# One tuned kernel for two transformer layers: convolution taps spread over three stages, the first merge chunk in the attention's drain, squares rounded on ScalarE

## What is computed

```python
def first_block(x, ...):
    h = rmsnorm(x, norm1_g)
    u, v_a, q, k, v_b = split(h @ w_in)
    y_a = chunked_spatial_gating(u, v_a, ...)
    o = diff_attention(q, k, v_b, lam, slopes)          # 8 heads, two maps each
    y_b = rmsnorm(o, sub_norm_g) * (1.0 - lam_init)     # over 128 elements of a head
    g_a, g_b = split(sigmoid(h @ w_gate + b_gate))
    x = x + (g_a * (y_a @ w_up_a) + g_b * (y_b @ w_up_b)) @ w_out
    return x + hierarchical_moe(rmsnorm(x, norm2_g), ...)   # 32 experts, 2 of them a token

def hybrid_layer(x, mem, ...):
    q_nsa, kv_nsa, g_nsa, conv_in, q_mem, g_merge = split(rms_norm(x, norm_mix) @ w_in)
    # NSA: compressed blocks (kc, vc), selected blocks, window; q_nsa normalised by head
    kc = rms_norm(compress_blocks(k_c, ...), nsa_qk_norm[1])
    o_nsa = nsa_attention(q, kc, vc, ks, vs, kw, vw, sigmoid(g_nsa))
    # convolution over time, 31 taps, each channel by itself
    u = a * sigmoid(ag)
    u = depthwise_conv(u, conv_w, 31 taps) + conv_b
    br_conv = silu(layer_norm(u, ...)) @ w_conv_out
    # attention to 256 memory rows, 4 heads of 128
    br_mem = softmax(qm @ km.T * 128 ** -0.5) @ vm @ w_mem_out
    gm = sigmoid(g_merge)                               # three gates of width 1024
    h = x + (gm[0] * br_nsa + gm[1] * br_conv + gm[2] * br_mem) @ w_out
    hn = rms_norm(h, norm_ffn)
    return h + (silu(hn @ w_gate) * (hn @ w_up)) @ w_down
```

## Time and profile before

| what | us |
|---|---|
| median of three executions (lowest, highest) | 1798.85 (1795.72, 1800.32) |
| the execution that was profiled, its own time | 1797.08 |
| span of that profile, first to last instruction | 1795.5 |
| TensorE busy in it | 1752.4 |
| VectorE, GpSimd, ScalarE busy | 877.8, 752.6, 579.6 |
| mean granted clock of TensorE, as a share of full speed | 0.991 |

### The profile page before, as it was taken

One profiled execution on the slowest core, in us unless ns is written; L12 is line 12 of the kernel. 1 busy time (PEld: TensorE's weight loads), 2 busy tenths in 40 slices (PEclk: granted clock), 3 DMA queues, 4 the chain that ended last, 5 costly groups with the idle time before them and its releaser, 6 DMA issues.

```text
span 1795.5 us, 22939 instructions
## 1 busy us (share of the span) xinstructions
PE 1752.4 (98%) x8545; PEld 1308.2 (73%) x8545; DVE 877.8 (49%) x1322; ACT 579.6 (32%) x1084; POOL 752.6 (42%) x623
## 2 busy tenths in 40 slices
PE   9999999998999999999999899999999999999999
PEld 6888877776887444443688677777788788888887
DVE  4221886667663244332552679997467442112211
ACT  2323445544233111111241345555462222212220
POOL 4444434334450000000341468887635545544442
PEclk9999999999999999999999999999999999999999
DMA  6322232224343899999722422221354223222221
GB/s 230 101 83 94 83 100 71 89 89 147 103 144 130 282 403 369 389 401 383 285 87 64 148 82 81 73 71 53 106 199 148 94 85 103 94 94 94 97 91 47
DMA packets 82935, 264.25 MB, mean 147 GB/s; under 512 B 9360, under 2 KB 10384, under 8 KB 82832
## 3 DMA queue, kind: packets, MB, share of 16 engines
q1 hardware_dynamic: 64608, 230.31, 36.5%
q10 hardware_dynamic: 15920, 28.32, 4.5%
q0 software_dynamic: 2304, 4.20, 0.7%
HBM read 249.16 MB, written 17.83 MB: 149 GB/s over the span
## 4 chain that ended last, share of the span: by engine, by line
PE 87%; DVE 9%; DMA 2%; ACT 1%; issue 1%; POOL 1%; SPq 0%; ACTq 0%; POOLq 0%; DVEq 0%
PE psum L620 84%; DVE area L2131 2%; DMA more<-stream 1%; DVE area L2190 1%; DVE negm L2171 1%; PE psum L1018 1%; DVE gh L2204 1%; PE psum L750 1%; DVE area L2704 1%; DVE area_r L2074 0%; PE psum L1394 0%; DVE den L2200 0%; DVE gh L2198 0%; ACT area L1559 0%; DVE area_r L2073 0%
## 5 line engine op out<-in xcount | busy, mean ns | idle before, releaser
L620 PE MATMUL psum<-area_r,ring_hi 128*128 128x512 f32 x3104 | 973.6, 395 | 4.6 <-DVE area_r L2074 1.4
L496 POOL TENSOR_TENSOR ring_lo<-ring,ring_hi 128x512 fp32r<-128x512 f32 x420 | 564.3, 1366 | 784.9 <-ACT ring_hi L1559 780.2
L620 PEld LDWEIGHTS psum<-area_r,ring_hi 128*128 128x128 f32 x3104 | 576.7, 188 | 130.9 <-issue 14.2
L620 PE MATMUL psum<-area_r,ring_lo 128*128 128x512 f32 x1552 | 606.2, 391 | 0.0
L1559 ACT ACTIVATE ring_hi<-ring 128x1024 fp32r<-128x1024 f32 x210 | 221.6, 1059 | 552.1 <-PE psum L620 515.6
L620 PEld LDWEIGHTS psum<-area_r,ring_lo 128*128 128x128 f32 x1552 | 291.9, 188 | 62.5
L1559 ACT ACTIVATE area<-psum 128x512 f32<-128x512 f32 (+3 forms) x252 | 124.0, 518 | 232.0 <-PE psum L750 73.7
L620 PE MATMUL psum<-ring,area 128*64 128x512 f32 (+1 forms) x480 | 135.9, 605 | 1.7 <-DMA ring<-stream 1.5
L620 PE MATMUL psum<-area 128*64 128x128 f32 (+7 forms) x864 | 113.6, 340 | 6.4 <-DVE negm L2180 4.6
L2074 DVE TENSOR_TENSOR area_r<-area,area_r 128x512 fp32r<-128x512 f32 x90 | 104.6, 1162 | 3.1
L552 POOL DMA_INDIRECT area<-tokens,idx x16 | 16.2, 1012 | 200.2 <-DVE idx L2437 155.0
(11 more groups left out here) (246 smaller groups left out, 1580.7 us busy)
## 6 DMA issues: line engine op xcount, KB each, us to landing
ring<-stream SPq DMA_DIRECT2D x324, 512.0 KB
more<-stream SPq DMA_DIRECT2D x48, 1024.0 KB
gates<-root ACTq DMA_DIRECT2D x24, 256.0 KB, 2.0
area<-gates SPq DMA_DIRECT2D x24, 256.0 KB, 6.0
gates<-area ACTq DMA_DIRECT2D x20, 256.0 KB, 4.1
area<-gates ACTq DMA_DIRECT2D x20, 256.0 KB, 5.3
area<-xT SPq DMA_DIRECT2D x8, 256.0 KB, 4.4
area<-xT ACTq DMA_DIRECT2D x8, 256.0 KB, 3.6
```

Of the source, the lines that this page charges most:

```text
L496: ins = nc.gpsimd.tensor_tensor(ring_lo[:, c % RS, n], ring[:, c % R, n], ring_hi[:, c % RS, n].bitcast(F32), ALU.subtract)
L620: return nc.tensor.matmul(out, lhsT, rhs, start=first, stop=last)
```

## The change

1. In the diff attention `tail` is now called in each drain pass. In the first one it does merge1's chunk 0, with a wait for each step's part of YA. The merge's own loop runs over chunks 1 to 7; the head sums come behind chunk 2, the spreads behind 3 and 4.
2. ACT squares each head twice, once rounded into YBH's tile and once in full into `ONSQ`; DVE subtracts once instead of casting and subtracting. Three gate products, not two, stand ahead of the normalisation on DVE.
3. The wait for `cmp_out` goes from ACT's first q2 square to PE's first head sum.
4. DVE's 62 taps: 17 ahead of `kc` (was 30), one behind each of q2's eight heads, 24 in NSA behind the scaled probabilities (was 32, ahead of the compressed maxima), 13 in the memory attention. POOL's 62 steps start in q2, one behind each of eight chunks' low parts, then 2.5 a chunk, instead of three ahead of each gate2 chunk's low part.
5. Half of the first gate2 chunk of the memory attention stands in the pass behind NSA's last unit, a quarter chunk behind each of two pairs of transposes. `MEM_FILL` is moved up by half a chunk, and three chunks, not two, go by thirds.

```diff
@@ -264,8 +264,8 @@
         G2_NSA, G2_MEM = 1, 17
-        MEM_FILL = [(u // 2, 4 * (u % 2), 4 * (u % 2) + 4) for u in range(10)]
-        MEM_FILL += [(x, lo, min(lo + 3, KD)) for x in (5, 6) for lo in (0, 3, 6)]
+        MEM_FILL = [((u + 1) // 2, 4 * ((u + 1) % 2), 4 * ((u + 1) % 2) + 4) for u in range(7)]
+        MEM_FILL += [(x, lo, min(lo + 3, KD)) for x in (4, 5, 6) for lo in (0, 3, 6)]
         for name in ("va_sq", "va_ss", "va_root", "v_out", "u_out", "z_mm", "bank_read", "lam_e",
@@ -586,9 +586,6 @@
                 low(split_no(c) + 1, c)
-            split(CMP1, C0["gate2"] + RS)
-
-            pool.wait_ge(S("conv_u"), CONVT)
@@ -603,11 +600,15 @@
-            for n in range(3 * KD):
-                for s in range(3 * n, min(3 * n + 3, 2 * TAPS)):
+            for c in range(CMP1, CMP1 + RS):
+                low(split_no(c) + 1, c)
+            pool.wait_ge(S("conv_u"), CONVT)
+            done = 0
+            for n, c in enumerate(range(CMP1 + RS, C0["gate2"] + RS + 3 * KD)):
+                low(split_no(c) + 1, c)
+                for s in range(done, min(n + 1 if n < 8 else 8 + (n - 7) * 5 // 2, 2 * TAPS)):
                     conv_step(s)
-                c = C0["gate2"] + RS + n
-                low(split_no(c) + 1, c)
+                    done = s + 1
             split(C0["merge2"] + RS, NCHUNK)
@@ -680,6 +681,8 @@
                     n, mat = entries[j][2], entries[j][5]
+                    if name == "q2" and j == 0:
+                        pe.wait_ge(S("cmp_out"), 4)
                     pe.wait_ge(S("hdsq"), b0 + j + 1)
@@ -718,8 +721,8 @@
                 for u in range(len(units) + 3):
-                    if u == len(units) and tail is not None:
-                        tail()
+                    if u >= len(units) and tail is not None:
+                        tail(u - len(units))
                     if u < len(units):
@@ -856,7 +859,13 @@
-            attention("diff", fill=fill1)
+            def merge_first(x):
+
+                if x == 0:
+                    pe.wait_ge(S("de"), 2 * len(score_items("diff")[0]) - 3)
+                    by_tile(C0["merge1"], 0, waited(YAH, YAL, S("ya_split"), 0, True))
+
+            attention("diff", fill=fill1, tail=merge_first)
@@ -867,19 +876,18 @@
-            pe.wait_ge(S("ya_split"), 8)
-            for m in range(KD):
-                if m == 2:
+            for m in range(1, KD):
+                if m == 3:
                     for h in range(8):
...
                         mm(psum[0:8, 6, :], pick[:, 7 - h:15 - h], tr(ONSQ[h]), False, h == 7).then_inc(S("onsum"), 1)
-                elif m == 3:
+                elif m == 4:
                     pe.wait_ge(S("on_rec"), 2)
...
                     pe.wait_ge(S("bank_read"), 8 + m - 3)
-                if m == 4:
+                if m == 5:
                     spread(4, 8)
@@ -1337,8 +1345,6 @@
                         S("cmp_mm"), 1)
-                elif j == 2:
-                    pe.wait_ge(S("cmp_out"), 4)
@@ -1427,9 +1433,13 @@
                         gate2(G2_NSA + u, (x + 4, x + 5))
+                    elif x < 4 and u == len(NSA_UNITS):
+                        gate2(G2_MEM, (x, x + 1))
             pe.wait_ge(S("nov"), 4)
-            def conv_sum():
-
+            def conv_sum(x):
+
+                if x:
+                    return
                 pe.wait_ge(S("me"), 16)
@@ -1699,6 +1709,7 @@
                 act.wait_ge(S("dov"), j + 1)
+                A(tr(YBH + j), tile(Q + j), ACT.Square)
                 A(tile(ONSQ[j]), tile(Q + j), ACT.Square).then_inc(S("onsq"), 1)
@@ -1941,7 +1952,6 @@
                 S("cmp_root"), 1)
-            act.wait_ge(S("cmp_out"), 4)
             normed("q2", q2_entries())
@@ -2211,9 +2221,9 @@
                         nsa_cscaled(u - 1)
-                    conv_taps(30 + 2 * u, 32 + 2 * u)
                     nsa_cmaxima(u)
                     nsa_scaled(u)
+                    conv_taps(25 + 24 * u // 16, 25 + 24 * (u + 1) // 16)
                 nsa_cscaled(len(NSA_UNITS) - 1)
@@ -2274,7 +2284,8 @@
                 dve.wait_ge(S("onsq"), h + 1)
-                split(tr(YBH + h), tr(ONSQ[h]), tile(ONSQ[h])).then_inc(S("onout"), 1)
+                V.tensor_tensor(tr(ONSQ[h]), tile(ONSQ[h]), tr(YBH + h).bitcast(F32), ALU.subtract).then_inc(
+                    S("onout"), 1)
             dve.wait_ge(S("onroot"), 1)
@@ -2284,15 +2295,15 @@
-            gated(0, 0)
-            gated(0, 1)
+            for m in range(3):
+                gated(0, m)
             for h in range(8):
...
                 split(tr(YBH + h), tr(YBL + h), tile(Q + h)).then_inc(S("onout"), 1)
-            for m in range(2, KD):
+            for m in range(3, KD):
                 gated(0, m)
@@ -2627,7 +2638,7 @@
             dve.wait_ge(w_lo, split_no(CMP1 + 1) + 1)
-            conv_taps(14, 30)
+            conv_taps(14, 17)
             dve.wait_ge(S("cmp_root"), 1)
@@ -2635,7 +2646,8 @@
                                        op0=ALU.mult, op1=ALU.mult).then_inc(S("cmp_out"), 1)
-            normed("q2", q2_entries(), lambda j, to: tile(to))
+            normed("q2", q2_entries(), lambda j, to: tile(to),
+                   between=lambda j: conv_taps(17 + 1 * j, 17 + 1 * (j + 1)))
             nsa()
@@ -2647,7 +2659,12 @@
-            attention("mem", between=splits)
+            def mem_between(u):
+
+                splits(u)
+                conv_taps(min(49 + u, 2 * TAPS), min(49 + u + 1, 2 * TAPS))
+
+            attention("mem", between=mem_between)
             dve.wait_ge(S("ln_sum"), 1)
...
                 V.scalar_tensor_tensor(out=tile(CV + c), in0=psum[:, 3, :], scalar=-1.0 / (CONVT * P), in1=tile(CV + c),
```

## The result

The changed kernel takes 1781.46 us in the median of four executions (1777.54 to 1783.12), the kernel before 1799.59 (1795.72 to 1800.84, four). The ratio is 0.990, with an interval of 0.9877 to 0.9922, so it is faster, by 18.1 us against some 20 that were forecast (20.4 from the traces). The profiled execution took 1781.04, its span is 1779.4.

A forecast was written before the change was run, and what follows sets the result against it. TensorE was taken as the bound, busy 1752.4 of 1795.5 us; in NSA VectorE is nearly full too. 6.3 + 8.7 + 3.9 + 1.8 - 0.3 = 20.4 us off 1797.08 gave 1776.7, stated as 1777, range 1770 to 1787.

The forecast's parts named there:

- B: Start of q2: fewer taps ahead of kc end TensorE's wait and half clock; 8.7 us won (6.5 to 9.5).
- C: NSA: 24 taps for 32, behind the scaled probabilities, end five waits; 3.9 us won (-1 to 5).
- D: End of NSA: half a gate2 chunk between the last transposes covers waits; 1.8 us won (1 to 2.7).
- A: Drain of the first attention and merge behind it: early chunk fills waits; 6.3 us won (4 to 7).
- The drain's 7.1 us: First attention's drain: second merge chunk begins 7.1 us earlier, 4.6 of it waits and some 2.5 clock.
- a wait of 0.6 us at merge1's last chunk: Merge: TensorE would reach the last chunk at 457.6 and wait 0.6 us for one product.
- the 0.2 us for the root: Merge: ScalarE's root for on_rec may start 0 to 1 us late, behind gate loads; taken as 0.2.
- E: Memory attention: 13 units get a VectorE tap, a loss of 0.3 us (0 to 3).
- Rival 1: NSA: VectorE stays the bound, taps beside GpSimd being dear; C gives nothing, E may lose 2; 1782 us, 11%.
- Rival 2: Drain and q2: the full clock does not come back, 2.5 + 1.9 us lost; 1781 us, 9%.
- Rival 3: NSA: first maxima behind the taps put every tap on TensorE's path; slower than before, 1815 us, 3%.
- rival 4: Waits move: GpSimd's last taps or gate loads late, at convolution's sum or merge1's fifth chunk; 1787 us, 7%.

The follow-up runs named there:

- experiment 1: Changed kernel with VectorE's merge reordered: one gate product, heads 0 to 3 normalised at one stretch, three gate products, then the four splits; 1775.65 us.
- experiment 9: Changed kernel with experiment 1's merge order, a fifth tap ahead of kc, other taps, memory-attention splits and gate table rearranged; 1772.88 us.
- experiment 5: Changed kernel with GpSimd's work as before: no convolution step in q2, three ahead of each gate chunk's low part; 1781.09 us.
- Experiment 11: Changed kernel with 32 NSA taps ahead of the compressed maxima, five in the memory attention, none beside a split, GpSimd's new rate kept; 1781.24 us.
- experiments 3: Changed kernel with the memory attention's gate chunks as before: no half chunk behind the last NSA unit, old table; 1780.76 us.
- experiment 8: Changed kernel with taps out of the four units with a split and gate chunks as before; 1777.61 us.
- Experiments 2: Changed kernel with the memory attention's 13 taps moved: four behind the last NSA unit, none in the four units with a split; 1779.33 us.

## Why the prediction held, and where its steps failed

The time lies 4.5 us above the forecast and inside the range. By the profiled executions it is 1781.04 for 1776.7, 4.3 us: two misses on the same side, 2.65 and 3.2, less 1.5 us won beyond the forecast in B, C, D and elsewhere.

**A, mis-sized: 6.3 forecast, 3.65 measured.** The drain's 7.1 us came to within 0.15; the timeline shows it, and no run undid the early chunk. The step that failed is what follows it: I counted a wait of 0.6 us at merge1's last chunk and called the third gate product free. I had not looked at the second spread's own wait on head 3. Before, it found that normalisation just done; now TensorE came 1.9 us earlier, VectorE did one gate product more ahead of it, and a cast took 1.46 us where it had taken 0.81. That gave 2.07 us of wait and 1.7 of half clock, and experiment 1 gave them back. The 0.6 us at the last chunk and the 0.2 us for the root never came; the former since TensorE was late itself.

**B, right in size and for the most part in cause: 8.7 and 8.8.** The wait of 7.21 us and the half clock went. That the taps ahead of kc set its start is borne out by experiment 9, where a fifth brings 0.88 us of wait back; no run put ACT's wait for `cmp_out` back alone, so its share is not shown. The wait for the last head grew by 0.42 us, forecast 0.4. But the tap that costs it is dear by GpSimd's low part, not by its convolution steps (experiment 5).

**C, right in size; the cause named was enough, but not needed: 3.9 and 4.5.** I put the gain down to eight taps less and to their place. Experiment 5 has both without GpSimd's new rate: the waits for the compressed maxima are gone and the later groups take 43.44 us, as forecast (43.5). Experiment 11 has neither, and GpSimd's rate, which I had only as an argument against a rival, does 4.1 us by itself. So the waits had two cures, and from the changed kernel alone nothing could be said of the cause. I also wrote that I am wrong if compressed scores wait in NSA, and gave 0.3 us to the first unit and 0.1 to a group. They waited once, for the exponentials of the third unit:

```profile
1072.01 0.41 PE L621 MATMUL psum<-kc,area 64*128 64x31 f32 x4 [0.77 <-ACT area L1568]
```

That is the step I had named, at about its price (0.7 us over the stage). It grew to 2.4 us with GpSimd's old rate (experiment 5). The taps' own cost was overrated: they were priced at 1.43 us and take 0.83 in the mean behind the scaled probabilities.

**D, right in size: 1.8 and 2.2.** The half chunk that I gave as the cause is worth 1.3 of it (experiments 3 and 8); the other 0.9 were not forecast and their cause is open.

**E, the step that failed: 0.3 forecast, 3.5 measured**, above my bound of 3. I read VectorE's 24.3 of 57.0 us, an average over 16 units, and priced the four units with a split at 4.1 us. They take 4.6 to 5.6: the tap takes 1.77 us where I had 1.47 at most, and with it in the unit three of the four casts take 1.5 us, which took 0.42 before. In experiment 8, without taps in these units, all four take 0.42 again, and in experiment 5, with GpSimd as before, they take 1.5. So the casts became dear with VectorE's taps, not with GpSimd's new steps. And I gave the moved table no price at all, though it moves ScalarE's copies into other units. Experiments 2, 3 and 8 show both.

**The rivals.** Rival 1 named GpSimd slowing VectorE, in NSA first, where its steps became fewer. There it did not strike. In the memory attention, where rival 1 put a loss of 2 us, it did, through VectorE's own taps; GpSimd's new steps are 0.4 of the 3.5 us (experiment 5). Rival 2 failed: the clock came back in the drain and in q2. Rival 3 is refuted: with 32 taps at the new place NSA still is 3.4 us shorter than before. Of rival 4, neither the gate loads nor the convolution's sum was late: no wait of TensorE is put down to either.
